# Two transformer blocks on one core: row transfers issued ahead of GpSimd's gating, squares on ScalarE, two narrow stages reordered, last blocks normalised in wide operations

## The reference, cut to what matters

```python
y_intra = jnp.einsum('bgij,bghij,bjghp->bighp', cb, decay, x_c)
...
y = y + xs.astype(jnp.float32) * d_skip.astype(jnp.float32)[:, None]
...
g = y.astype(jnp.float32) * jax.nn.silu(z.astype(jnp.float32))
gs = gs * lax.rsqrt(jnp.mean(jnp.square(gs), axis=-1, keepdims=True) + EPS)
...
y = (xf - mu) * lax.rsqrt(var + LN_EPS)
return (y * g.astype(jnp.float32) + b.astype(jnp.float32)).astype(x.dtype)
```

## Time and profile before

| | us |
|---|---|
| median of 3 runs (lowest, highest) | 1493.3 (1493.2, 1494.57) |
| the profiled execution, its own time | 1496.57 |
| its span (first to last instruction) | 1494.8 |
| TensorE busy in the span | 1467.8 |
| VectorE, ScalarE, GpSimd busy | 1103.1, 834.8, 184.8 |
| mean granted clock of TensorE | 0.995 |

### The profile page before, as it was taken

One profiled execution on the slowest core, in us unless ns is written; L12 is line 12 of the kernel. 1 busy time (PEld: TensorE's weight loads), 2 busy tenths in 40 slices (PEclk: granted clock), 3 DMA queues, 4 the chain that ended last, 5 costly groups with the idle time before them and its releaser, 6 DMA issues.

```text
span 1494.8 us, 25448 instructions
## 1 busy us (share of the span) xinstructions
PE 1467.8 (98%) x10183; PEld 1359.8 (91%) x10183; DVE 1103.1 (74%) x1461; ACT 834.8 (56%) x1144; POOL 184.8 (12%) x169
## 2 busy tenths in 40 slices
PE   9999999999999999999999999999999999999997
PEld 7999998999988899888999988889988899988887
DVE  7778997887987757666596687665976558886654
ACT  5655567655655446555464566544655445665533
POOL 0110003562000010000130030001300013030001
PEclk9999999999999999999999999999999999999999
DMA  8957756645555755555544344555555554445552
GB/s 345 370 211 282 251 201 249 212 161 170 208 188 197 275 178 196 188 181 193 197 170 169 141 169 172 193 197 181 186 182 184 196 193 146 170 173 192 197 184 70
DMA packets 43368, 295.93 MB, mean 198 GB/s; under 512 B 5020, under 2 KB 7196, under 8 KB 8718
## 3 DMA queue, kind: packets, MB, share of 16 engines
q1 hardware_dynamic: 40542, 280.24, 52.0%
q0 software_dynamic: 2736, 14.41, 2.7%
HBM read 291.44 MB, written 3.19 MB: 197 GB/s over the span
## 4 chain that ended last, share of the span: by engine, by line
PE 82%; DVE 9%; ACT 3%; issue 2%; DMA 2%; POOL 2%; ACTq 0%; SPq 0%; DVEq 0%; POOLq 0%
PE banks L707 30%; PE banks L709 15%; PE banks L722 4%; PE banks L725 4%; PE banks L724 4%; PE banks L897 4%; PE banks L899 4%; PE banks L900 4%; DVE deep_lo L1887 3%; PE banks L794 1%; PE banks L793 1%; PE banks L795 1%; DMA raw<-in_panels 1%; DMA rows<-cum_rows 1%; PE banks L916 1%
## 5 line engine op out<-in xcount | busy, mean ns | idle before, releaser
L1887 DVE TENSOR_TENSOR deep_lo<-raw,deep_hi 128x1024 fp32r<-128x1024 f32 x386 | 462.3, 1245 | 108.4 <-ACT deep_hi L1320 104.5
L707 PE MATMUL banks<-H,deep_hi 128*128 128x512 f32 x1504 | 522.4, 392 | 2.2 <-DVE H L2135 1.4
L1320 ACT ACTIVATE deep_hi<-raw 128x1024 fp32r<-128x1024 f32 x386 | 381.9, 1047 | 145.7 <-DMA raw<-in_panels 139.8
L709 PE MATMUL banks<-H,deep_lo 128*128 128x256 f32 x1504 | 420.4, 280 | 0.0
L707 PEld LDWEIGHTS banks<-H,deep_hi 128*128 128x128 f32 x1504 | 282.3, 188 | 65.7 <-issue 1.6
L709 PEld LDWEIGHTS banks<-H,deep_lo 128*128 128x128 f32 x1504 | 282.3, 188 | 0.0
L1887 DVE TENSOR_TENSOR w_lo<-raw,w_hi 128x1024 fp32r<-128x1024 f32 x104 | 138.1, 1339 | 50.6 <-ACT w_hi L1320 50.4
L707 PE MATMUL banks<-HH,deep_hi 128*128 128x512 f32 x480 | 166.6, 392 | 0.0
L1320 ACT ACTIVATE w_hi<-raw 128x1024 fp32r<-128x1024 f32 x104 | 109.1, 1057 | 82.1 <-PE banks L900 59.9
L897 PE MATMUL banks<-H,w_lo 128*128 128x256 f32 x512 | 146.7, 287 | 1.5 <-ACT gate_a L1551 1.5
L899 PE MATMUL banks<-H,w_hi 128*128 128x256 f32 x512 | 144.7, 283 | 0.0
(11 more groups left out here) (368 smaller groups left out, 2847.5 us busy)
## 6 DMA issues: line engine op xcount, KB each, us to landing
raw<-in_panels SPq DMA_DIRECT2D x265, 1024.0 KB, 4.8
rows<-cum_rows POOLq DMA_DIRECT2D x16, 384.0 KB, 4.3
late_w<-in_panels POOLq DMA_DIRECT2D x4, 1024.0 KB, 6.4
bias_rows<-rev POOLq DMA_DIRECT2D x1, 2048.0 KB, 15.3
XS<-in_x_t SPq DMA_DIRECT2D x2, 512.0 KB, 5.1
near<-bias_rows POOLq DMA_DIRECT2D x8, 128.0 KB, 2.7
out_t<-XS SPq DMA_DIRECT2D x4, 256.0 KB, 2.6
ws<-in_ws_t POOLq DMA_DIRECT2D x1, 512.0 KB, 12.4
```

The source lines that it names most:

```text
L707: pe.matmul(bank, high(place)[:, at:at + P], operand[:, kk, :, :].rearrange("p a t -> p (a t)"), start=starts and c == chunks[0], stop=False)
L709: return pe.matmul(bank[:, 0:T], low(place)[:, at:at + P], operand[:, kk, 0, :], start=False, stop=stops and c == chunks[-1])
L1320: act.activation(high(sl)[:, w], raw[:, r, w], ACT.Copy).then_inc(panel_hi, 1)
L1887: vec.tensor_tensor(low(sl)[:, w], raw[:, r, w], high(sl)[:, w], ALU.subtract).then_inc(panel_lo, 1)
```

## The change

Four edits in one diff.

1. Scan, GpSimd: the loop goes in steps of two. In each step the addition of an older group's squares comes first, then both row transfers, then both gatings. The squares are no longer made on GpSimd. `y_lo` of groups 0 to 2 is done in one place (n = 14). Scan, ScalarE: a new `squared(g)` squares two blocks in one operation of 512 columns, at odd n from 3 on, and the last one behind the first branch panel. `decay_gaps` of the next two steps goes behind the splits of the odd step.
2. "out" and "pool_out": a `narrow_stage` on ScalarE and on VectorE in place of `stage`/`stage_x`. ScalarE splits the fifth panel ahead of the first group's squares; VectorE splits it ahead of `add_block` 1 to 3 and of the four `unscaled_lo`.
3. "att_out": VectorE's split of panel q, first half, comes ahead of the variance, as for the other stages.
4. The last norm: `last_norm` on VectorE takes off the mean in one operation for blocks 2 and 3 and one for blocks 4 to 7, multiplies by the root in two operations of 1024 columns, and does weight and bias of blocks 4 to 7 in one two-scalar operation each. ScalarE does weight and bias of blocks 0 to 3. SyncE writes the pairs 0, 4, 2, 6 in this order.

```diff
-            for g in range(4):
-                sp.wait_ge(S["norm_x"], KD * 5 + 2 * (g + 1))
-                two = slice(2 * g, 2 * g + 2)
+            for at in (0, 4, 2, 6):
+                if at < BANKS:
+                    sp.wait_ge(S["norm_x"], KD * 5 + at + 2)
+                else:
+                    sp.wait_ge(S["out_ready"], at - BANKS + 2)
+                two = slice(at, at + 2)
...
             def gating(m):
                 pool.wait_ge(S["y_skip"], m + 1)
                 pool.tensor_tensor(xbc[:, m, :], xbc[:, m, :], z_t[:, m, :], ALU.mult).then_inc(S["y_gated"], 1)
-                pool.wait_ge(S["y_gated"], m + 1)
-                if m >= 4:
-                    pool.wait_ge(S["y_sums"], m // 2 - 1)
-                pool.tensor_tensor(sq[:, m % 4, :], xbc[:, m, :], xbc[:, m, :], ALU.mult).then_inc(S["y_sq"], 1)
             def squares_added(g):
                 at = 2 * (g % 2)
-                pool.wait_ge(S["y_sq"], 2 * (g + 1))
+                pool.wait_ge(S["y_sq"], g + 1)
                 pool.tensor_tensor(sq[:, at, :], sq[:, at, :], sq[:, at + 1, :], ALU.add).then_inc(S["y_added"], 1)
...
-            for n in range(PAIRS):
-                if n >= 2 and n % 2 == 0:
+            for n in range(0, PAIRS, 2):
+                if n >= 4:
+                    squares_added((n - 4) // 2)
+                for r in range(2):
+                    if n + r + ROW_SLOTS < PAIRS:
+                        pool.wait_ge(S["exp_done"], n + r + 1)
+                        rows_in(n + r + ROW_SLOTS)
+                if n:
                     gating(n - 2)
-                if n + ROW_SLOTS < PAIRS:
-                    pool.wait_ge(S["exp_done"], n + 1)
-                    rows_in(n + ROW_SLOTS)
-                if n >= 2 and n % 2:
-                    gating(n - 2)
-                    squares_added((n - 3) // 2)
-                if n == 7:
+                    gating(n - 1)
+                if n == 6:
                     pool.wait_ge(S["c_rowed"], 1)
                     pool.wait_ge(S["cb_done"], 4)
                     pool.tensor_copy(c_late, c_row[:, :]).then_inc(S["c_moved"], 1)
-                if n >= 13:
-                    y_lo(n - 13)
+                if n == PAIRS - 2:
+                    y_lo(0)
+                    y_lo(1)
+                    y_lo(2)
+            squares_added(SSM_GROUPS - 2)
...
+            def narrow_stage(name):
+                s = INDEX[name]
+                q = FIRST_PANEL[s]
+                for p in (2, 3, 4):
+                    split(q + p, *raw_place(q + p))
+                squares_post(s, 0, FIRST_GROUP[s] % 2)
+                split(q + 5, *raw_place(q + 5))
+                squares_post(s, 1, 1 - FIRST_GROUP[s] % 2)
...
+            def squared(g):
+                at = 2 * (g % 2)
+                act.wait_ge(S["y_gated"], 2 * (g + 1))
+                if g >= 2:
+                    act.wait_ge(S["y_sums"], g - 1)
+                act.activation(sq[:, at:at + 2, :], xbc[:, 2 * g:2 * g + 2, :], ACT.Square).then_inc(S["y_sq"], 1)
...
-                elif n + 1 < PAIRS:
-                    decay_gaps(n + 1)
-                    decay_gaps(n + 2)
...
+                if n % 2 and n + 1 < PAIRS:
+                    decay_gaps(n + 1)
+                    decay_gaps(n + 2)
+                if n % 2 and n >= 3:
+                    squared((n - 3) // 2)
...
+                if n == 0:
+                    squared(SSM_GROUPS - 1)
...
-                    for m in range(KD):
-                        act.wait_ge(S["norm_y"], KD * norms[0] + m + 1)
-                        act.activation(xb[:, m, :], xb[:, m, :], ACT.Identity, bias=cols[:, at + m:at + m + 1])\
-                            .then_inc(S["norm_x"], 1)
+                    act.wait_ge(S["norm_y"], KD * norms[0] + BANKS)
+                    for m in range(BANKS):
+                        g = COLS["ln_g"] + KD * (norms[0] - 3) + m
+                        act.activation(xb[:, m, :], xb[:, m, :], ACT.Identity, bias=cols[:, at + m:at + m + 1],
+                                       scale=cols[:, g:g + 1]).then_inc(S["norm_x"], 1)
...
+            def narrow_stage(name, new_x, biased=0):
+                s = INDEX[name]
+                q, G = FIRST_PANEL[s], FIRST_GROUP[s] % 2
+                for p in (2, 3):
+                    split(q + p, *raw_place(q + p))
+                if biased:
+                    vec.wait_ge(S["norm_x"], KD * biased)
+                products_done(s, 0)
+                for b in range(BANKS):
+                    last = new_x(b, banks[:, BANKS * G + b, 0:T])
+                last.then_inc(taken, 1)
+                split(q + 4, *raw_place(q + 4))
+                for m in (1, 2, 3):
+                    add_block(name, m)
+                for m in range(BANKS):
+                    unscaled_lo(name, m)
+                split(q + 5, *raw_place(q + 5))
+                last_group(name, 1, 1 - G, new_x)
...
+            def last_norm(k, stage_name, i):
+                def repeated(t, blocks):
+                    return t.unsqueeze(1).to_broadcast([P, blocks, T])
+                def taken_off(first, n):
+                    part_x = xb[:, first:first + n, :]
+                    vec.tensor_tensor(part_x, part_x, repeated(banks[:, stat_bank(stage_name), 0:T], n), ALU.subtract)\
+                        .then_inc(S["norm_centred"], n)
+                taken_off(2, 2)
+                taken_off(4, 4)
+                vec.wait_ge(S["stat_root"], k + 2)
+                for g in range(2):
+                    vec.wait_ge(S["norm_centred"], KD * (k - 3) + BANKS * (g + 1))
+                    half = by_group(xb)[:, g, :, :]
+                    vec.tensor_tensor(half, half, repeated(st[:, 2, :], BANKS), ALU.mult).then_inc(S["norm_y"], BANKS)
+                vec.wait_ge(S["norm_y"], KD * (k + 1))
+                for m in range(BANKS, KD):
+                    scale, bias = COLS["ln_g"] + KD * i + m, COLS["ln_b"] + KD * i + m
+                    vec.tensor_scalar(xb[:, m, :], xb[:, m, :], cols[:, scale:scale + 1], cols[:, bias:bias + 1], ALU.mult,
+                                      ALU.add).then_inc(S["out_ready"], 1)
...
-                    if stage_name != "att_out":
-                        split_half(q, 0)
+                    split_half(q, 0)
...
-                    if stage_name == "att_out":
-                        split_half(q, 0)
```

More of the change, by code:

```diff
@@ L338, in two_blocks @@
             "pt_done pt_copied o_done o_hi o_lo "
-            "pool_hi pool_lo pool_f pads_clear pool_block pool_kept pool_y_hi pool_y_lo inv_loaded x_stored").split()}
+            "pool_hi pool_lo pool_f pads_clear pool_block pool_kept pool_y_hi pool_y_lo inv_loaded out_ready x_stored").split()}
         block = ctx.enter_context(nc.Block())
@@ L1723, in _ @@
                     y_hi(4 + HIDDEN_BEHIND.index(n))
-            stage("out", squares_post)
+            narrow_stage("out")
             act.wait_ge(S["c_kept"], 1)
@@ L1862, in _ @@
             pool_scaled(1, POOL_BLOCKS[2:])
-            stage("pool_out", squares_post)
+            narrow_stage("pool_out")
             feed_forward(3, last=True)
@@ L2049, in take_up @@
                     last.then_inc(taken, 1)
-                    if name not in SUMMED_AHEAD:
-                        for m in (1, 2, 3):
-                            add_block(name, m)
                 def split_and_low(q, *place, halves=(0, 1)):
@@ L2509, in _ @@
                         mixed_rest(g, half)
-            stage_x("out", gated_x(16))
+            narrow_stage("out", gated_x(16))
             stage("ff1", relu2_post, first_group("out", 1, ev8, mod[:, 24:32], first_relu2))
@@ L2528, in layer_norm @@
                 variance(k + 1, True, LN_EPS, stage_name)
+                if last:
+                    last_norm(k, stage_name, i)
+                    return
                 apply_norm(k, xb, cols[:, COLS["ln_g"] + at:COLS["ln_g"] + at + KD],
@@ L2674, in _ @@
             pool_scaled(1)
-            stage_x("pool_out", deep_x, norms[0] - 3)
+            narrow_stage("pool_out", deep_x, norms[0] - 3)
             feed_forward(3, 5, last=True)
```

## The result

The changed kernel takes **1484.1 us** (median of 5, 1483.3 to 1486.8), against 1493.3 (1492.9 to 1494.6) for the kernel before on the same chip: ratio 0.9942, 95% interval 0.9931 to 0.9953. That is 9.2 us faster (by the interval 7.0 to 10.3); 11.6 were forecast. The profiled execution took 1483.95 (span 1482.2). In what follows, "a profile" is one execution. The first one of experiment e8 ran at a mean granted clock of 0.75, so its stage times are not used and that kernel was profiled once more (e8b).

What follows compares the result with a forecast made beforehand. TensorE, busy 98%, was taken as the bound, so only its waits and the tail could give: 6.0 + 1.2 + 1.7 + 1.5 + 0.5 + 0.7 = 11.6 us, from the median 1493.3 to 1481.7, range 1479.0 to 1488.5.

Steps and rivals of the forecast that it cites:

- Scan, 6.0: Scan: earlier row transfers, ScalarE's splits first and squares off GpSimd gain 6.0 of 8.4 us; bounds 0 and 8.4.
- The 1.2 held back: Scan: 1.2 us taken off for a square ahead of ScalarE's exponentials and GpSimd's three `y_lo` together at n = 14.
- "out", 1.2: "out": the next panel's split ahead of the sums fills VectorE's idles and removes TensorE's wait at L815; 1.2 us gained.
- "pool_out", 1.7: "pool_out": the same move as in "out" cuts TensorE's wait of 1.83 us by 1.7.
- att_out", 0.5: "att_out": VectorE's split ahead of the variance brings the centring 1.1 us earlier; 0.5 us gained, bounds 0 and 1.1.
- Clock, 1.5: Behind "pool_out": the lower granted clock goes with the wait; 1.5 us gained, bounds 0 and 1.7.
- rival 2: Behind "pool_out": the clock fall stays or comes at another wait; 1483.2 us, chance 0.10.
- Last blocks, 0.7: Last norm: the last result comes 0.8 us sooner, less 0.1 for closer transfers; 0.7 us gained, bounds 0.2 and 0.9.
- From profile to median: Whole kernel: the median of the runs lies 3.27 us below the profiled execution, so 1485.0 becomes 1481.7.
- (1): Rival: ScalarE becomes the scan's bound, so the scan gives 2.0 us; 1485.7 us, chance 0.18.
- (3): Rival: Square is not loaded, so five scan squares each cost ScalarE two table loads; 1484.7 us, chance 0.05.
- (4): Rival: the scan's rows loop grows and makes the kernel slower; 1511 us at 16 us a pair, chance 0.03.

Runs made afterwards that it cites:

- e8: Changed kernel with blocks 0 to 3 multiplied before the mean comes off blocks 4 to 7, and pairs written 0, 2, 4, 6: 1485.85 us.
- e3: Kernel before with the scan edits alone, but the squares left on GpSimd, each behind its gating: 1489.5 us, ratio 0.9966.
- e4: Kernel before with only the squares moved to ScalarE, one instruction for two blocks: 1492.2 us, ratio 0.9984.
- e5: Kernel before with only ScalarE's row gaps put behind its weight splits; GpSimd still issues rows late and does the squares: 1489.1 us, ratio 0.9968.

## Why the prediction was right, and where not

- **What bounds the kernel** held: only TensorE's waits and the tail moved.
- **Scan, 6.0:** 5.7 in the two profiles, 6.4 over all. The size is right, and so is the mechanism as far as ScalarE's queue goes (a split behind a wait for rows). It led with the transfers and with GpSimd's squares, and neither was needed for most of it: ScalarE's order alone has 5.0 of the 6.4 (149.9 to 144.9). What the transfers would give alone stays open. What was forecast to stay was wrong in one item: the roots at n = 11 were to leave 0.3, and left a period 1.4 too long. The 1.2 held back for ScalarE's queue and `y_lo` covered that, which is luck as far as the item goes.
- **"out", 1.2:** 1.0. **"pool_out", 1.7:** 2.2 in the two profiles, 1.8 over all. **"att_out", 0.5:** 0.7 in the two profiles, 0.4 over all. All within what one profile can tell.
- **Clock, 1.5:** this failed, on both of its assumptions. The fall mostly doesn't come with the wait (one profile of six has it), so the kernel's median hardly held it, as far as six profiles tell; and VectorE's chain covered it, so it was worth nothing. By the Trainium skill (TensorE: Matmul & The Clock Gate, The HAM clock gate), such changes vary by run; the thirteen profiles agree, at 72 to 84 us and here. The forecast weighed that rule as rival 2, at 0.10, and it was the better guide. A single occurrence behind the longest wait was no proof of a cause.
- **Last blocks, 0.7:** this failed, at -0.4 in the profile, of which 0.3 are its own. The working priced the last result (0.8, found 0.5: VectorE's four took 1.38 us together and not 1.12, and its first wide subtraction began 3.5 us after the last product on HH and not 3.4) and gave the transfers 0.1. They cost 0.95, 4.0 us from the last result to the end against 3.0.
- **From profile to median:** right, and for a reason that the trace of before had in its windows at 72 to 84 us.

Together: 11.6 - 1.6 (clock) - 1.1 (last blocks) and +0.2 from the rest are 9.1; 9.2 were measured. The forecast of 11.6 itself lies above the interval of 7.0 to 10.3: the range held, the sum was too high, and by the clock and the last blocks.

**Rivals.** (1) ScalarE's bound appeared in one period, for 1.4 us, not in all. (3) is out. The changed kernel's squares (minimum, median and maximum ns, first and last start) are

```profile
L1697 ACT ACTIVATE XS<-xbc x8: 613/617/620, 241.5 to 320.6; 128x512 f32<-128x512 f32 x8
```

and no table load stands beside any of them but the one that the roots ask for. (4) never came near: the period was 11.67. The rows took longer to land, though, a median of 5.4 us against 4.3, in e3 as well (5.3), not in e4 or e5 (4.4, 4.3); so this came with the earlier issue, and the slack took it. That GpSimd and VectorE shut each other out (the Trainium skill, SBUF — State Buffer, Who interferes with whom), the trace of before agrees with:

```profile
252.84 2.12 DVE L1887 TENSOR_TENSOR w_lo<-raw,w_hi 128x1024 fp32r<-128x1024 f32 x1
253.94 1.49 POOL L605 TENSOR_TENSOR XS<-xbc 128x256 f32<-128x256 f32 x1
254.88 1.36 DVE L2392 TENSOR_TENSOR ev<-ev,cb 128x768 f32<-128x768 f32 x1
```

Five of the 16 squares took 1.48 to 1.49 us, and these are the five that began while VectorE was making a low half; the others took 0.61 to 0.68. VectorE paid too: these low halves took 1.72 to 2.13 us, against 1.21 to 1.23 with GpSimd idle, and the decayed scores right behind them 1.36 against 0.94 to 0.96. But little came back. The scan's 37 low halves and 16 decayed scores took 71.3 to 75.9 us of VectorE in the four profiles of the old scan, 68.6 in e4 and 71.6 in the changed kernel. What the exclusion costs in time no run decides: the squares' move is worth 2.0 us alone and 0.7 with the rest, which the freed GpSimd queue may explain as well.

## What to carry to other kernels

In a queue executed in order, put the instruction that needs nothing new ahead of the one that waits for a transfer before making the transfer earlier; here that one swap of a few lines had 5.0 of 6.4 us (whether the earlier transfer alone would have had as much was not measured). Before pricing a stretch at a lower clock or a filled wait, ask which engine's chain ends behind it, and see in a second profile whether it comes again. For a tail that ends in transfers, add up when each can start and not only when the last result is ready.

## What was not expected of the hardware

- The granted clock fell to 0.50 with TensorE busy for the whole of the window (72 to 84 us), in 4 of 13 profiles, and stayed at 1.00 behind waits of 1.5 to 1.7 us in five. It also fell right behind a wait of 1.8 us in one profile and of 2.0 us in another, and behind the last product in all.
- GpSimd's squares took 1.48 us and not 0.61 when they began beside a VectorE low half, and that low half up to 2.13 us and not 1.21; in the changed kernel VectorE's sum over the scan was hardly less.
- The median landing of the 384 KB row transfers went from 4.3 to 5.4 us when they were issued earlier, nothing else about them being changed.
- Four output transfers of 256 KB took 4.0 us beyond the last result when issued within 2.25 us, 3.0 when issued within 3.75.
